# A hybrid diffusion trunk on one core: attention behind eight projection halves instead of twelve, sixteen halves in thirds between its steps, the mod group among the scan's levels

## The chip, the cores and the metric

One core of a Trainium2 chip runs the whole program. The metric is the device time of one execution in microseconds (us), the median of several runs.

## The reference, cut to what matters

Two token groups, 128 context tokens and 256 latent tokens on a 4 x 64 grid, go together (384 tokens) through two layers. A layer is a half-step SwiGLU, a token mixer and another half-step SwiGLU; each is normed before and after and modulated by shift, scale and gate from a conditioning vector. The first layer's mixer, the even mixer, is what the change touches:

```python
a_q, a_ff, a_fb, a_i, a_g, b_q, b_k, b_v = split_even(h @ w_in)      # 8 parts of 512 columns
o_a, _ = hgrn2_mixer(a_q, a_ff, a_fb, a_i, a_g, lb, gnorm, s_ctx)    # 4 heads, forward and backward gated scan
o_b = neighbourhood_attention(b_q, b_k, b_v, k_ctx, v_ctx, rpb)      # 8 heads of 64, softmax with a bias table
out = concatenate([o_a, o_b], axis=-1) @ w_out
```

For the context tokens the attention is a plain softmax over 128 keys; for the latent tokens the keys are the 256 latent ones in a window plus 128 cached ones. The new keys and values of the context tokens are outputs (cache_k_new, cache_v_new), as are the final scan states.

## The kernel before, in words

**Matmuls in three terms.** Everything is float32 with products in fp32r: each operand is split into a high part (rounded) and a low part (the rest), and a product is high x high + high x low + low x high. A weight tile is 1024 x 256; its two column halves are *halves*, numbered by tau (tile tau // 2). ScalarE makes a half's high part (L400, `split_act`), VectorE then its low part (L414, `split_dve`), and TensorE runs 24 matmuls (8 chunks x 3 terms, L445 to L447, `pe_half`). High and low parts have room for four halves, so the split of half tau + 4 waits until half tau is used. ScalarE's and VectorE's `proj(tau)` therefore each start with the split for the tile two ahead (`ahead`). For the value parts (a_i and b_v, parts 3 and 7) the tokens are the rows of the result: TensorE takes both halves of a tile at once (L1830 to L1832; it needs both low parts), and ScalarE evicts and splits the next tile's two halves only at the odd tau.

**Loads.** SyncE's DMA queue loads weight tiles of 1 MB into a ring of 6 in the order of `ring_order`; a slot's next load waits until its tile was split or, for a mod tile, used.

**Order of the even mixer's parts.** `AB_ORDER` is the order of the 16 column tiles: b_q (4 halves), b_k (4), b_v (4), then the scan's two forget parts, its query, a_i and a_g. Halves 0 to 3 run as the stage's first four, 4 to 11 by a loop, with these between them: the transposes of the cached keys (behind half 5), two pairs of slots of the mod group modC (behind 6 and 8; each 64 small matmuls, L1591), the transposes of the new context keys KP into bank 7 (behind 8), and modC's turn (behind 10). For b_q and b_k, VectorE also subtracts the high copy from the bank to get the low part (`proj_low`: BQL L1300 and L1301, KPL and BKL L1304 and L1305; semaphore proj_lo). ctx_lo (L1335) is the same for the cached keys: VectorE does it in its loop at tau 7, behind its proj(7).

**Attention steps.** The 24 units u are 8 heads x 3 query blocks. TensorE's step s runs: the scores of units s and s + 1 if s is even (L1873), the values (P x V) of step s - 3 at u % 6 of 1 or 5 (L1881, L1888), the transposes of unit s - 2 (L1918, they wait for p_ready and for the previous copy), then a part of a projection half. VectorE's step s adds the bias (L1347), takes the maximum (L1351) and scales it (L1354) for u = s, then takes the reciprocal and scales the weights of u = s - 1 (L1359, L1361), then runs its proj. ScalarE copies the transposed weights of s - 2 (L924), takes the exponent of u = s (L929), and runs its proj. Twelve halves (12 to 23) are spread over the steps, one half over two steps, 12 matmuls each, in banks 0 and 1 by turns. In step 16 ScalarE also runs four sigmoids over the forget parts (`gate_sigmoids`, L889 and L891), each side of them a table load; halves 20 and 21 run whole in steps 16 and 17, and steps 18 and 19 have none. VectorE scales the sigmoids (`gate`, L1318 and L1320) at the end of step 17 and clamps (L1324) in steps 20 and 22.

**Levels.** Behind the steps come the diagonal products and seven levels of the scan (L1931, L1964). Each level: ScalarE joins keys (L950), TensorE multiplies, VectorE updates keys, queries and totals (L1412, L1417, L1401). A projection half (24 to 31) stands behind each level. Heads, output projection and turnover follow.

Of the kernel before, what the change touches and what calls it, by code (L numbers as in the profile page):

```python
# [45 lines left out]
SIGMOIDS = (16,)  # L46
# [60 lines left out]
MOD_BANK = {6: 6, 7: 5, 8: 6, 12: 6, 16: 6, 17: 6}  # L107
# [27 lines left out]
def ring_order():  # L135
# [5 lines left out]
    for s in range(6):  # L141
# [3 lines left out]
        if kind == "even":  # L145
            order += run(f"in{s}", 2, 6) + run("modC", 0, 2) + run(f"in{s}", 6, 7) + run("modC", 2, 4)
            order += run(f"in{s}", 7, 16) + run(f"out{s}", 0, 4)
# [35 lines left out]
def trunk(nc, x_prompt, x_sample, c, state_hgrn, cache_k, cache_v, c_ctx, mod_w, mod_b, norm_pre, norm_post,  # L183
# [5 lines left out]
    with ctx:  # L189
# [20 lines left out]
        LMASK = sb("LMASK", [P, LEVELS * P], I32)[:, 0:INNER * BLK].rearrange("p (l t) -> p l t", l=INNER)  # L210
# [49 lines left out]
        KP = SUMS[:, 0:512].rearrange("p (a b) -> p a b", a=4)  # L260
# [123 lines left out]
        AB_ORDER = [10, 11, 12, 13, 14, 15, 2, 3, 4, 5, 0, 1, 6, 7, 8, 9]  # L384
# [125 lines left out]
        def ab_bank(tau):  # L510

            return bank[tau % 4 if tau < 12 else tau % 2 if tau < 24 else 4 + tau % 4]
# [15 lines left out]
        def attention_proj(step):  # L528

            part = 4 * (step % 2)  # L530
            if any(step in (at, at + 1) for at in SIGMOIDS):
                return 12 + step // 2 + step % 2, range(KD)
            if any(step in (at + 2, at + 3) for at in SIGMOIDS):
                return None
            return 12 + step // 2, range(part, part + 4)
# [61 lines left out]
        def _(pool):  # L597
# [35 lines left out]
            pool.wait_ge(kout_turned, 1)  # L633
            pool.wait_ge(mod_turned, turned_before(first_group("modC")) + 1)
# [26 lines left out]
        def _(act):  # L661
# [184 lines left out]
            def even(s):  # L846
# [47 lines left out]
                for tau in range(12):  # L894
# [7 lines left out]
                    if tau == 9:  # L902
                        act.wait_ge(kout_turned, 1)
                        act.activation(KOUT, bank[7][:], ACT.Copy).then_inc(kout_ready, 1)
                        act.wait_ge(kout_ready, 1)
                        act.dma_start(cache_k_new[0, 0].rearrange("h t d -> t h d"),
                                      KOUT.rearrange("p (h d) -> p h d", h=HEADS_B)).then_inc(k_stored, 16)
                        mod_rows_out(g0)
                mod_cols_out(g0)
                act.wait_ge(proj_out, 12)  # L910
                act.dma_start(cache_v_new[0, 0].rearrange("h t d -> t h d"),
                              BV[:, 0, :].rearrange("p (h d) -> p h d", h=HEADS_B)).then_inc(v_stored, 16)
                for step in range(24 + 3):
                    u = step - 2
                    if 0 <= u < 24:
                        n = NT if head_block(u)[1] else P
                        act.wait_ge(p_turned, u + 1)
                        if u == 0:
                            act.wait_ge(k_stored, 16)
# [17 lines left out]
                    if 2 <= step <= 24 and step % 2 == 0:  # L937
                        proj(11 + step // 2)
                    if step in SIGMOIDS:
                        gate_sigmoids(0)  # L940
                        gate_sigmoids(1)
# [12 lines left out]
                for lv in range(LEVELS):  # L954
                    join(lv)
                    if lv == 0:
                        act.wait_ge(diag_mm, 3)
                        act.activation(ATTD, level_bank(2)[:, 0:UNITS * BLK].rearrange("p (u t) -> p u t", u=UNITS),
                                       ACT.Copy).then_inc(diag_out, 1)
                    if lv == 6:  # L960
# [5 lines left out]
                    proj(24 + lv)  # L966
                act.wait_ge(lvl_mm, 3 * LEVELS)
# [22 lines left out]
                for h in range(HEADS_A):  # L990
# [6 lines left out]
                    act.wait_ge(o_mm, h + 1)  # L997
                    if h >= 2:
# [63 lines left out]
        def _(dve):  # L1062
# [223 lines left out]
            def even(s):  # L1286
# [8 lines left out]
                def proj_low(tau):  # L1295
                    part, q = divmod(AB_ORDER[tau // 2] * 2 + tau % 2, 4)
                    B = bank[tau % 4]
# [29 lines left out]
                for tau in range(12):  # L1327
# [9 lines left out]
                for step in range(24 + 1):  # L1337
# [748 lines left out]
```

## Time and profile before

| what | us |
|---|---|
| median of 3 runs | 1601.13 (1598.25 to 1602.56) |
| profiled execution, its time | 1599.43 |
| its span | 1597.4 |
| TensorE matmul busy | 1543.8 |
| VectorE busy | 1085.6 |
| ScalarE busy | 688.0 |
| even mixer: first four halves end, attention starts, levels start, levels end | 343, 385, 467, 518 |

Times in the trace count from the start of the span. In a timeline row the first number is the start, the second the length; a matmul's length is more than its distance to the next one, since they are pipelined. A bracket at the end of a row gives the idle time of the engine before it and what ended it. The clock of TensorE is the share of 2.4 GHz that was granted.

### The profile page before, as it was taken

The page shows a single profiled execution, that of the slowest core. Times are in us where ns is not written, and L with a number is a line of the kernel's source. Part 1 is how long each engine was busy: PE and PEld are TensorE (multiplying, and loading weights), DVE is VectorE, ACT ScalarE, POOL GpSimd, SP SyncE. Part 2 cuts the span into 40 slices and gives each one's busy share as a digit, 9 for nine tenths or more (in the row PEclk, how much of TensorE's full clock was granted, in tenths as well). Part 3 has the DMA queues.
Part 4 walks back from the last instruction along what each step waited for, and adds up shares of the span by engine and source line. Part 5 has one row for each costly group of instructions (what it writes and reads, how often), then busy time and mean ns, then how long its engine had stood idle before and what let it go on. Part 6 is the DMA issues. An engine that isn't in the chain of part 4 may idle for free.

```text
span 1597.4 us, 26083 instructions
## 1 busy us (share of the span) xinstructions
PE 1543.8 (97%) x10631; PEld 1508.4 (94%) x10631; DVE 1085.6 (68%) x1975; ACT 688.0 (43%) x1202; POOL 50.3 (3%) x50
## 2 busy tenths in 40 slices
PE   5999999999989899999999999999999999999999
PEld 4999999989868889999999999999999989999999
DVE  5678889774679887878946788885553885344332
ACT  4433334464556574333334533334453265333333
POOL 2000000002102000000000000000000000000000
PEclk9999999999999999999999999999999999999999
DMA  9765656567321265655645455654453354443311
GB/s 326 249 201 169 199 184 224 185 218 217 94 89 55 79 199 165 204 185 179 201 149 193 159 176 192 197 189 161 142 182 126 106 181 137 132 133 125 104 62 39
DMA packets 255654, 259.77 MB, mean 163 GB/s; under 512 B 6625, under 2 KB 253842, under 8 KB 255538
## 3 DMA queue, kind: packets, MB, share of 16 engines
q1 hardware_dynamic: 250528, 253.25, 49.1%
q10 hardware_dynamic: 4114, 2.84, 0.6%
q0 software_dynamic: 896, 2.06, 0.5%
q8 instruction: 82, 1.34, 0.4%
q14 instruction: 34, 0.28, 0.0%
HBM read 255.50 MB, written 2.62 MB: 162 GB/s over the span
## 4 chain that ended last, share of the span: by engine, by line
PE 83%; DVE 9%; ACT 3%; issue 3%; POOL 1%; ACTq 0%; DMA 0%; DVEq 0%; POOLq 0%
PE bank L445 25%; PE bank L446 24%; PE bank L447 24%; DVE PARTS L1123 1%; DVE WL L414 1%; PE bank L467 1%; PE bank L1649 1%; ACT WH L400 1%; PE bank L469 1%; PE bank L468 1%; DVE X L1189 1%; DVE HL L1152 1%; DVE SUMS L1454 1%; POOL WL L414 1%; PE bank L1830 1%
## 5 line engine op out<-in xcount | busy, mean ns | idle before, releaser
L414 DVE TENSOR_TENSOR WL<-RAW,WH 128x1024 fp32r<-128x1024 f32 (+1 forms) x335 | 398.5, 1194 | 420.4 <-ACT WH L400 419.6
L400 ACT ACTIVATE WH<-RAW 128x1024 fp32r<-128x1024 f32 (+1 forms) x344 | 357.5, 1043 | 607.0 <-PE bank L447 593.3
L445 PE MATMUL bank<-HH,WH 128*128 128x384 f32 x1664 | 564.5, 339 | 7.9 <-DVE WL L414 3.5
L447 PE MATMUL bank<-HH,WL 128*128 128x384 f32 x1664 | 561.0, 337 | 0.0
L446 PE MATMUL bank<-HL,WH 128*128 128x384 f32 x1664 | 560.9, 337 | 0.0
L445 PEld LDWEIGHTS bank<-HH,WH 128*128 128x128 f32 x1664 | 314.7, 189 | 10.0 <-issue 3.9
L446 PEld LDWEIGHTS bank<-HL,WH 128*128 128x128 f32 x1664 | 314.5, 189 | 0.0
L447 PEld LDWEIGHTS bank<-HH,WL 128*128 128x128 f32 x1664 | 314.4, 189 | 0.0
L445 PE MATMUL bank<-AH,WH 128*128 128x384 f32 x704 | 237.4, 337 | 0.0
L447 PE MATMUL bank<-AH,WL 128*128 128x384 f32 x704 | 237.0, 337 | 0.0
L446 PE MATMUL bank<-AL,WH 128*128 128x384 f32 x704 | 237.0, 337 | 0.0
L1123 DVE SCALAR_TENSOR_TENSOR SUMS<-RAW,COND,SUMS 128x256 f32<-128x256 f32 x420 | 176.2, 478 | 0.0
L445 PEld LDWEIGHTS bank<-AH,WH 128*128 128x128 f32 x704 | 132.8, 189 | 0.1
L446 PEld LDWEIGHTS bank<-AL,WH 128*128 128x128 f32 x704 | 132.8, 189 | 0.0
L447 PEld LDWEIGHTS bank<-AH,WL 128*128 128x128 f32 x704 | 132.8, 189 | 0.0
L828 ACT ACTIVATE AH<-TT 128x384 fp32r<-128x384 f32 x88 | 45.6, 519 | 108.8 <-DVE TT L1261 108.8
L467 PE MATMUL bank<-HH,WH 128*128 128x384 f32 x192 | 66.8, 348 | 4.5 <-DVE HL L1152 2.9
L469 PE MATMUL bank<-HH,WL 128*128 128x384 f32 x192 | 64.8, 337 | 0.0
L468 PE MATMUL bank<-HL,WH 128*128 128x384 f32 x192 | 64.7, 337 | 0.0
L741 ACT ACTIVATE HH<-TT,MOD,CA 128x128 fp32r<-128x128 f32 x96 | 47.3, 540 | 33.3 <-DVE TT L1138 31.8
L1123 DVE SCALAR_TENSOR_TENSOR PARTS<-RAW,COND,PARTS 128x256 f32<-128x256 f32 x140 | 56.3, 478 | 0.0
L414 POOL TENSOR_TENSOR WL<-RAW,WH 128x1024 fp32r<-128x1024 f32 x9 | 21.4, 2393 | 1085.9 <-ACT WH L400 876.6
(249 smaller groups left out, 1465.0 us busy)
## 6 DMA issues: line engine op xcount, KB each, us to landing
RAW<-in_ffn_w_in SPq DMA_DIRECT2D x88, 1024.0 KB, 5.1
RAW<-in_mod_w SPq DMA_DIRECT2D x72, 1024.0 KB, 5.0
RAW<-in_ffn_w_out SPq DMA_DIRECT2D x32, 1024.0 KB, 5.1
RAW<-in_ab_w_in SPq DMA_DIRECT2D x16, 1024.0 KB, 6.4
RAW<-in_ffn_w_out SPq DMA_DIRECT2D x16, 768.0 KB, 4.5
RAW<-in_cv_w_in SPq DMA_DIRECT2D x12, 1024.0 KB, 5.2
RAW<-in_ab_w_out SPq DMA_DIRECT2D x4, 1024.0 KB, 5.1
RAW<-in_cv_w_out SPq DMA_DIRECT2D x4, 1024.0 KB, 5.2
```

The costliest lines, as they stand in the source:

```text
L400: e.activation(WH[:, (2 * m + b) % 4, 0:nk, :], RAW[:, p, 0:nk, b * P:(b + 1) * P], ACT.Copy).then_inc(half_hi, 1)
L414: e.tensor_tensor(WL[:, k, 0:nk, :], RAW[:, p, 0:nk, b * P:(b + 1) * P], WH[:, k, 0:nk, :].bitcast(F32), ALU.subtract).then_inc(half_ready, 1)
L445: e.matmul(out, WH[:, k, kk, :], xh(kk), start=(first and kk == 0), stop=False)
L446: e.matmul(out, WH[:, k, kk, :], xl(kk), start=False, stop=False)
L447: mm = e.matmul(out, WL[:, k, kk, :], xh(kk), start=False, stop=(last and kk == nk - 1))
L467: e.matmul(outs[b], WH[:, kh[b], kk, :], HH[:, kk, :], start=False, stop=False)
L468: e.matmul(outs[b], WH[:, kh[b], kk, :], HL[:, kk, :], start=False, stop=False)
L469: e.matmul(outs[b], WL[:, kh[b], kk, :], HH[:, kk, :], start=False, stop=False)
L741: a = act.activation(HH[:, d, t0:t1], TT[:, d % 2, t0:t1], ACT.Identity, bias=MOD[:, 24 * s + d, g:g + 1], scale=CA[:, s, d, g:g + 1])
L828: act.activation(AH[:, bass.ds(i * 6 + (j + b), 1), :], TT[:, 2 + b:3 + b, :], ACT.Copy).then_inc(act_hi, 1)
L1123: x = dve.scalar_tensor_tensor(a[:, g, :], w, by, a[:, g, :], ALU.mult, ALU.add)
L1152: dve.tensor_tensor(HL[:, d, :], TT[:, 2 + d % 2, :], HH[:, d, :].bitcast(F32), ALU.subtract).then_inc(h_ready, 1)
```

## The change

The order of the tiles becomes b_q and b_k of the first four heads (halves 0 to 3), b_v (4 to 7), b_q and b_k of the other four heads (8 to 11), then as before. Attention starts behind half 7. Sixteen halves (8 to 23) run between its steps: in steps 0 to 17 two halves over three steps (18, 15 and 15 matmuls), halves 20 and 21 whole in steps 18 and 19, 22 and 23 in two parts each in steps 20 to 23. Banks 0 and 1 take turns from half 8 on, and halves 10 to 13 also wait for the low part of the half two before. The sigmoids move to step 18 (ScalarE), the gates to step 19, the clamps to 21 and 23 (VectorE). The mod group's pairs move behind levels 0 and 2, its turn behind level 4, in bank 3; the transposes of KP stand behind half 24, and KP gets a place of its own. POOL's bias loads wait for the cached keys' transposes instead of the new keys'. The ring's order follows.

```diff
-SIGMOIDS = (16,)
+SIGMOIDS = 18
-MOD_BANK = {6: 6, 7: 5, 8: 6, 12: 6, 16: 6, 17: 6}
+MOD_BANK = {6: 6, 7: 3, 8: 6, 12: 6, 16: 6, 17: 6}
-            order += run(f"in{s}", 2, 6) + run("modC", 0, 2) + run(f"in{s}", 6, 7) + run("modC", 2, 4)
-            order += run(f"in{s}", 7, 16) + run(f"out{s}", 0, 4)
+            order += run(f"in{s}", 2, 13) + run("modC", 0, 2) + run(f"in{s}", 13, 14) + run("modC", 2, 4)
+            order += run(f"in{s}", 14, 16) + run(f"out{s}", 0, 4)
-        KP = SUMS[:, 0:512].rearrange("p (a b) -> p a b", a=4)
+        KP = MASK_AREA[:, INNER * BLK:INNER * BLK + 512].bitcast(F32).rearrange("p (a b) -> p a b", a=4)
-        AB_ORDER = [10, 11, 12, 13, 14, 15, 2, 3, 4, 5, 0, 1, 6, 7, 8, 9]
+        AB_ORDER = [10, 12, 14, 15, 11, 13, 2, 3, 4, 5, 0, 1, 6, 7, 8, 9]
-            return bank[tau % 4 if tau < 12 else tau % 2 if tau < 24 else 4 + tau % 4]
+            return bank[tau % 4 if tau < 8 else tau % 2 if tau < 24 else 4 + tau % 4]
+        def fill(step):
+            if step >= SIGMOIDS + 2:
+                part = 4 * (step % 2)
+                return [(12 + step // 2, range(part, part + 4))]
+            if step >= SIGMOIDS:
+                return [(2 + step, range(KD))]
+            m, r = divmod(step, 3)
+            return [[(8 + 2 * m, range(0, 6))], [(8 + 2 * m, range(6, 8)), (9 + 2 * m, range(0, 3))],
+                    [(9 + 2 * m, range(3, 8))]][r]
+        def filled(step):
+            if step > SIGMOIDS + 2:
+                return [11 + step // 2] if step % 2 == 0 else []
+            if step > SIGMOIDS:
+                return [1 + step]
+            m, r = divmod(step - 2, 3)
+            return [8 + 2 * m + r] if step >= 2 and r < 2 else []
...
-            pool.wait_ge(kout_turned, 1)
-            pool.wait_ge(mod_turned, turned_before(first_group("modC")) + 1)
+            pool.wait_ge(ctx_turned, 1)
+            pool.wait_ge(mod_turned, turned_before(first_group("modC")))
...
-                for tau in range(12):
+                for tau in range(8):
                     proj(tau)
...
-                    if 2 <= step <= 24 and step % 2 == 0:
-                        proj(11 + step // 2)
-                    if step in SIGMOIDS:
+                    for tau in filled(step):
+                        proj(tau)
+                    if step == SIGMOIDS:
                         gate_sigmoids(0)
                         gate_sigmoids(1)
...
                     proj(24 + lv)
+                    if lv == 3:
+                        mod_rows_out(g0)
+                    if lv == 5:
+                        mod_cols_out(g0)
...
-                    if 2 <= step <= 24 and step % 2 == 0:
-                        proj(11 + step // 2)
-                    if step - 1 in SIGMOIDS:
+                    for tau in filled(step):
+                        proj(tau)
+                        if AB_ORDER[tau // 2] // 2 in (5, 6):
+                            proj_low(tau)
+                    if step == SIGMOIDS + 1:
                         for w in range(2):
                             dve.wait_ge(sig_done, 2 * w + 1)
                             gate((KFW, KBW)[w], w, k=True)
...
-                    if step in (20, 22):
-                        clamp((FF, FB)[step // 2 - 10])
-                    if step == 4:
-                        coefficients(g0)
+                    if step in (SIGMOIDS + 3, SIGMOIDS + 5):
+                        clamp((FF, FB)[(step - SIGMOIDS) // 2 - 1])
...
+                    if lv == 6:
+                        coefficients(g0)
...
                     else:
-                        pe.wait_ge(proj_out, tau - 1 if tau in range(14, 24) else tau - 3)
-                    if tau in range(4, 12):
+                        pe.wait_ge(proj_out, tau - 1 if tau in range(10, 24) else tau - 3)
+                    if tau in range(4, 8):
                         pe.wait_ge(proj_lo, tau - 3)
+                    if tau in range(10, 14):
+                        pe.wait_ge(proj_lo, tau - 5)
...
-                for tau in range(4, 12):
+                for tau in range(4, 8):
                     proj(tau)
...
-                    if tau in (6, 8):
-                        mod_pair("modC", tau - 6)
-                    if tau == 10:
-                        mod_turn(g0)
...
-                pe.wait_ge(proj_lo, 8)
+                pe.wait_ge(proj_lo, 4)
                 pe.wait_ge(ctx_lo, 1)
-                pe.wait_ge(kout_ready, 1)
...
+                        if u == 12:
                             pe.wait_ge(proj_out, 12)
-                            pe.wait_ge(mod_cols, g0 + 1)
+                            pe.wait_ge(proj_lo, 8)
...
-                    if step < 24 and attention_proj(step):
-                        proj(*attention_proj(step))
+                    for tau, steps in fill(step) if step < 24 else ():
+                        proj(tau, steps)
...
                 proj(24)
+                pe.wait_ge(ob_done, 4)
+                for ht in range(4):
+                    mm = pe.transpose(bank[7][:, ht * P:(ht + 1) * P], KP[:, ht, :], IDENT[:])
+                mm.then_inc(kout_turned, 1)
...
                     proj(25 + lv)
+                    if lv in (0, 2):
+                        mod_pair("modC", lv)
+                    if lv == 4:
+                        mod_turn(g0)
```

ScalarE's copy of the turned keys (KOUT) and its DMA to cache_k_new move from its tau 9 into level 0, and the wait for that store moves to the heads.

## Rows read from the trace of the kernel before

**Rows 1.** The page, busy time: engine, busy us, share of the span, instructions.

```profile
PE 1543.8 (97%) x10631; PEld 1508.4 (94%) x10631; DVE 1085.6 (68%) x1975; ACT 688.0 (43%) x1202; POOL 50.3 (3%) x50
```

**Rows 2.** Waits of TensorE, 343 to 518 us: us in total, times, longest.

```profile
PE bank L1918 <- DVE TT L1361: 4.8, 5, 2.0
PE bank L1931 <- ACT TT L950: 1.6, 1, 1.6
PE bank L445 <- DVE BQL L1301: 1.2, 1, 1.2
PE bank L1888 <- ACT SUMS L924: 1.1, 1, 1.1
PE bank L1918 <- ACT SUMS L924: 1.1, 1, 1.1
PE bank L1873 <- ACT MIX L859: 0.8, 1, 0.8
PE bank L1918 <- ACT SQ L924: 0.7, 1, 0.7
```

**Rows 3.** Windows: stretch, its length, busy us (instructions) per engine, clock, DMA.

```profile
445.00:450.00 5.00, 3.25 (x17) 2.04 (x19) 3.48 (x11) 3.92 (x11) 0.00 (x0) 0.72 0.00 0
...
495.00:500.00 5.00, 5.00 (x22) 5.00 (x21) 5.00 (x9) 3.33 (x5) 0.00 (x0) 0.66 0.41 135
...
550.00:555.00 5.00, 3.73 (x21) 3.20 (x20) 2.34 (x4) 3.64 (x8) 0.00 (x0) 1.00 0.00 0
```

**Rows 4.** Timeline of VectorE, 344 us: start, length, line, operands.

```profile
344.14 0.28 DVE L1300 TENSOR_TENSOR BQL<-bank,BQH 128x128 fp32r<-128x128 f32 x1
344.34 0.42 DVE L1301 TENSOR_TENSOR BQL<-bank,BQH 128x256 fp32r<-128x256 f32 x1
344.67 1.22 DVE L414 TENSOR_TENSOR WL<-RAW,WH 128x1024 fp32r<-128x1024 f32 x1
```

**Rows 5.** Timeline of TensorE and VectorE, attention's start, and the ctx_lo subtraction.

```profile
383.75 0.28 PE L1832 MATMUL bank<-WL,HH 128*128 128x256 f32 x1
...
385.91 2.36 DVE L414 TENSOR_TENSOR WL<-RAW,WH 128x1024 fp32r<-128x1024 f32 x2 [6.49 <-ACT WH L400]
...
367.10 0.68 DVE L1335 TENSOR_TENSOR BKL<-bank,BKH 128x512 fp32r<-128x512 f32 x1
```

**Rows 6.** Timeline, step 2: first scores, ScalarE's and VectorE's split.

```profile
389.65 0.45 PE L1873 MATMUL bank<-BKH,BQH 64*128 64x384 f32 x2
...
392.30 1.05 ACT L400 ACTIVATE WH<-RAW 128x1024 fp32r<-128x1024 f32 x1
...
393.38 1.23 DVE L414 TENSOR_TENSOR WL<-RAW,WH 128x1024 fp32r<-128x1024 f32 x1 [1.27 <-ACT WH L400]
```

**Rows 7.** Timeline around the sigmoids: a half's first and last matmul, ScalarE, VectorE.

```profile
438.26 0.42 PE L445 MATMUL bank<-HH,WH 128*128 128x384 f32 x1
...
442.33 0.34 PE L447 MATMUL bank<-HH,WL 128*128 128x384 f32 x1
...
436.48 1.28 ACT L889 ACT_TABLE_LOAD   x1
...
442.20 1.48 ACT L891 ACTIVATE MIX<-MIX 128x1536 f32<-128x1536 f32 x1
...
444.08 1.28 ACT L929 ACT_TABLE_LOAD   x1
...
439.30 1.41 DVE L1318 TENSOR_SCALAR MIX<-MIX,LBT 128x384 f32<-128x384 f32 x4 [0.31 <-ACT MIX L889]
...
443.72 1.65 DVE L1320 TENSOR_SCALAR MIX<-MIX,LBT 128x384 f32<-128x384 f32 x4
```

**Rows 8.** Timeline of TensorE, one pair of mod slots.

```profile
357.97 1.96 PE L1591 MATMUL bank<-RAW,COND 128*32 128x128 f32 x64
```

**Rows 9.** Windows, the levels, columns as in rows 3.

```profile
476.00:518.00 42.00, 39.55 (x821) 37.35 (x820) 40.14 (x69) 26.43 (x43) 8.17 (x4) 0.96 0.16 53
```

More of the change, by code:

```diff
@@ L209, in trunk @@
         ONES = sb("ONES", [P, P])
-        LMASK = sb("LMASK", [P, LEVELS * P], I32)[:, 0:INNER * BLK].rearrange("p (l t) -> p l t", l=INNER)
+        MASK_AREA = sb("LMASK", [P, LEVELS * P], I32)
+        LMASK = MASK_AREA[:, 0:INNER * BLK].rearrange("p (l t) -> p l t", l=INNER)
         WINDOW = sb("WINDOW", [P, GRID_W])
@@ L526, in weights_of @@
             return (SQ, SQ_ODD)[h % 2][:, (i + 1) % 2, :]
[L528 to L535, printed above, removed]
+        def fill(step):
[14 more added lines that the diff above has]
+            return [8 + 2 * m + r] if step >= 2 and r < 2 else []
         def two_halves(t, other, at, blocks, b, left=0, right=None):
@@ L901, in even @@
                                        ACT.Copy).then_inc(ctx_ready, 1)
[L902 to L910, printed above, removed]
+                act.wait_ge(proj_out, 8)
                 act.dma_start(cache_v_new[0, 0].rearrange("h t d -> t h d"),
@@ L917, in even @@
                         act.wait_ge(p_turned, u + 1)
-                        if u == 0:
-                            act.wait_ge(k_stored, 16)
                         if u % 6 >= 4:
@@ L959, in even @@
                                        ACT.Copy).then_inc(diag_out, 1)
+                        act.wait_ge(kout_turned, 1)
+                        act.activation(KOUT, bank[7][:], ACT.Copy).then_inc(kout_ready, 1)
+                        act.wait_ge(kout_ready, 1)
+                        act.dma_start(cache_k_new[0, 0].rearrange("h t d -> t h d"),
+                                      KOUT.rearrange("p (h d) -> p h d", h=HEADS_B)).then_inc(k_stored, 16)
                     if lv == 6:
@@ L997, in even @@
                     act.wait_ge(o_mm, h + 1)
+                    if h == 0:
+                        act.wait_ge(k_stored, 16)
                     if h >= 2:
@@ L1296, in proj_low @@
                     part, q = divmod(AB_ORDER[tau // 2] * 2 + tau % 2, 4)
-                    B = bank[tau % 4]
+                    B = ab_bank(tau)
                     dve.wait_ge(proj_out, tau + 1)
@@ L1326, in even @@
                 g0 = first_group("modC")
-                for tau in range(12):
+                for tau in range(8):
                     proj(tau)
@@ L1811, in proj @@
                     elif tau == 27:
-                        pe.wait_ge(ob_done, 4)
+                        pe.wait_ge(kout_ready, 1)
                     else:
-                        pe.wait_ge(proj_out, tau - 1 if tau in range(14, 24) else tau - 3)
-                    if tau in range(4, 12):
+                        pe.wait_ge(proj_out, tau - 1 if tau in range(10, 24) else tau - 3)
+                    if tau in range(4, 8):
                         pe.wait_ge(proj_lo, tau - 3)
+                    if tau in range(10, 14):
+                        pe.wait_ge(proj_lo, tau - 5)
                     part = AB_ORDER[tau // 2] // 2
@@ L1847, in even @@
                         mm.then_inc(ctx_turned, 1)
-                    if tau in (6, 8):
-                        mod_pair("modC", tau - 6)
-                    if tau == 10:
-                        mod_turn(g0)
-                    if tau == 8:
-                        pe.wait_ge(proj_out, 8)
-                        for ht in range(4):
-                            mm = pe.transpose(bank[7][:, ht * P:(ht + 1) * P], KP[:, ht, :], IDENT[:])
-                        mm.then_inc(kout_turned, 1)
-                pe.wait_ge(proj_lo, 8)
+                pe.wait_ge(proj_lo, 4)
                 pe.wait_ge(ctx_lo, 1)
-                pe.wait_ge(kout_ready, 1)
                 def scores(u):
@@ L1896, in even @@
                         if u == 0:
-                            pe.wait_ge(proj_out, 11)
+                            pe.wait_ge(proj_out, 7)
                         if u == 2:
+                            pe.wait_ge(proj_out, 8)
+                        if u == 12:
                             pe.wait_ge(proj_out, 12)
-                            pe.wait_ge(mod_cols, g0 + 1)
+                            pe.wait_ge(proj_lo, 8)
                         if u >= 4:
@@ L1907, in even @@
                         if u == 1:
-                            pe.wait_ge(proj_out, 12)
+                            pe.wait_ge(proj_out, 8)
                         if u % 6 == 1 and u > 1:
```

## The prediction, made before the changed kernel ran

> **What bounds the kernel now.** I read the page first, then who waited for whom on TensorE around the even mixer, then the timeline there, all engines side by side. TensorE is busy 97% of the span [rows 1], so a change of order can only change TensorE's idle time and its clock. In 343 to 518 us, from the mixer's fifth half to the end of its levels, that is little: the waits of [rows 2] sum to 11.3 us. Four (4.8 + 1.1 + 1.1 + 0.7 = 7.7 us) lie between attention steps, 0.7 of it in the early steps, 3.1 behind the sigmoids (1.1 and 2.0), 4.0 in the last steps. The other three: 1.2 before the fifth half, 0.8 before the first scores, 1.6 before level 3.
>
> The second loss is the clock. Behind the idle time of 443 to 447 us the granted clock is 0.72 for 5 us, behind the 1.6 us before level 3 it is 0.66 [rows 3]: a mix of the levels 2.4 and 1.2 GHz. Prices: 0.28 x 5 = 1.4 us, with the end of the drop 1.5, and 0.34 x 5 = 1.7 us. Yet in 550 to 555 us TensorE idles 1.3 us and the clock stays at 1.00 [rows 3], so a drop is likely and not sure.
>
> **The change, step by step.** TensorE's work stays the same: halves, scores, values, transposes and the mod group only change places. So I sum idle and slow time after minus before, over the same stretch. A half is 24 matmuls, 438.26 to the last start 442.33, that is 4.24 us with its switch; 12 more matmuls cost 2.1 us [rows 7].
>
> *A, the fifth half.* It becomes a V half, which needs both low parts of tile 2 instead of one. Before, TensorE left at the end of the first low-part subtraction, 344.76; the second split runs from 344.67 for 1.22 us [rows 4], so it leaves at 345.9. Price **+1.1**.
>
> *B, ctx_lo.* TensorE waits for ctx_lo before the first scores. VectorE issues it behind its proj(7). That tile is now V: its two low splits wait for ScalarE's two high splits, which wait for TensorE's half 7. Nothing is left in front of TensorE then. The same chain stands in the trace behind half 11: TensorE's last matmul 383.75 + 0.28 = 384.03, VectorE's pair of low splits ends at 385.91 + 2.36 = 388.27, 4.2 us later; the ctx_lo subtraction adds 0.68, less 0.1 of overlap [rows 5]. So 4.8 us of idle, where 0.8 stood [rows 2]. Price **+4.0**: four halves covered it before, nothing does now. From above 4.8, with no bound near 0, since every link of the chain is in the rows.
>
> *C, two banks.* Halves 8 to 11 used four banks and now use two, and two halves on wait for the low part (proj_lo) too. 16 matmuls a step are 2.8 us instead of 2.1. For half 10, due in step 3: from the scores of step 2 (389.65 before) ScalarE's split starts at 392.30 and VectorE's ends at 393.38 + 1.23 = 394.61 [rows 6]; the two BQL subtractions of half 8 add 0.6 [rows 4], so it is free 5.5 us after those scores start. TensorE is there after 0.7 + 0.1 + 2.6 + 0.1 = 3.5: idle 2.0. The same for half 12 (three evictions, then KPL and BKL) gives 0.7; halves 14 and 18, behind steps with the two output copies, about 0.6 and 0.5. Sum 3.8, before 0.7: **+3.1**. From below: halves 14 to 21 alternate in two banks before, without a wait before a half there in [rows 2], which gives -0.7; from above, twelve halves that wait 0.6 each give +6.5. I take the chain, since it follows the order of the queues. Perfetto Trace Analysis of the Trainium skill (Optimizing Tensor Performance, Matmuls) wants independent matmul groups to rotate through different PSUM banks so that evacuation overlaps: by it C is a loss, while by the quiet alternation of before the sum would be 3.8 us less.
>
> *D, the sigmoids.* They move from step 16 to 18, and halves 20 and 21 run whole beside them as before; the two empty steps behind are now filled with half 22. But VectorE's gates come behind its proj(20), the low split of tile 12's first half, and ScalarE makes the high split only in its step 19, behind all sigmoids. Before, the gates ran under the sigmoids: the first at 439.30, the last at 443.72 [rows 7]. Counted from the first table load S (436.48): sigmoids end at +7.2 (442.20 + 1.48), copy and second table load +8.9 (444.08 + 1.28) [rows 7], exponent of u=19 +9.4, high split +10.4, low split +11.6, the four groups of gates (1.41 + 1.65 twice, less overlaps, 5.9) +17.5, bias, maximum and scaling +18.9. Only then can TensorE transpose u=19 in step 21. In front of it TensorE has: half 21 to +6.1, scores to +6.9, values from +7.6 (when the copy is done and the second load starts) to +9.0, the first part of half 22 from +10.8 (half 20's eviction) to +12.9. Idle 0.7 + 1.8 + 6.0 = 8.5. The last steps keep their kind of wait; VectorE is as late as before and the clamps stand a step later: 4.1 for 4.0. So 12.6 idle after, against 7.0 idle and 1.5 of slow clock before: **+4.1**. Its own slow clock comes while ScalarE and VectorE set the pace and I let it vanish there. Bounds +1 (half 22 slow, so idle shrinks, and the tail closes) and +7 (clock not hidden). The page ScalarE: Activation LUTs of the Trainium skill (What ACT_TABLE_LOAD costs) adds a drain of 1.38 us to each switch. The rows disagree: from the load's end, 437.76, four sigmoids of 1.48 fill the time to 443.68. By the page D would be 2.8 us more.
>
> *E, clock.* The 4.8 us idle of B should bring the low clock to the first step, which TensorE bounds; price as in [rows 3], 1.5 to 1.7: **+1.6**, bounds 0 and +5 (a second drop behind the 2 us of C).
>
> *F, the levels.* The mod group's 128 small matmuls (1.96 us a pair, 1.9 start to start [rows 8]), its turn and the turn of KP move here: 4.5 us of TensorE work. VectorE is the other engine of the levels: 476 to 518 us has it busy 40.1 of 42 us, TensorE 39.6 [rows 9]. The second pair stands just before level 3 and covers its 1.6 us wait; with it the slow 1.7 goes: -3.3, less 0.2 for a thin VectorE lead: **-3.1**. Bounds -3.3 and 0: if VectorE stays later than TensorE, the new work is just added. ScalarE's copy of KOUT and the DMA issue behind it stand in front of join 1, which waits for level 0 anyway: 0.
>
> *Covered, so 0.* POOL starts its bias loads at ctx_turned, near 355, over 10 us before the second pair of scores. On SP the six weight tiles move two places forward, and modC's slots fall free at level 0, 10 us before tile 15 is split; if they were late, ScalarE's split in level 3 would wait. Mod coefficients are only needed by the turnover. k_stored is waited for some 40 us after its DMA.
>
> **Sum.** 1.1 + 4.0 + 3.1 + 4.1 + 1.6 - 3.1 = **+10.8**. The profiled execution took 1599.43 us (span 1597.4), so 1610.2. It stands 1.7 us under the median 1601.13, to which I carry the same difference: **1611.9**.
>
> **Rivals.**
> *R1, faster: the denser steps hide all.* With 16 matmuls a step no chain is late from step 3 to step 26: C -0.7, D -8.5, F -3.1, A and B +5.1, no E: -7.2, 1593.9. It decides at the transposes of u=19: they would have to be ready before the first part of half 22 ends, so the gates would have to run under the sigmoids. For it: one idle time of [rows 2] lies just there. Against: the order in VectorE's queue. Perfetto Trace Analysis of the Trainium skill (Optimization Strategy) says that interleaving regimes with different busiest engines may improve performance; that is this case. Chance 0.06.
> *R2, no change: B and A as said, the rest quiet.* C 0, D 0, E 0, F -3.1: +2.0, so 1603.1. For it: other halves alternate quietly in two banks. Chance 0.14.
> *R3, slower by more.* F gives nothing, since VectorE is full in the levels, and the low clock lasts (E +4): 10.8 + 3.1 + 2.4 = +16.3, 1617.4. For it: 40.1 of 42 us. Against: VectorE waits for level 0's matmuls even now. Chance 0.2.
> *The forecast:* chance 0.6.
>
> A measurement of this kernel tells about 0.3% from no change, 4.8 us. Low end: A and B +5.1, C 0, D +1, E 0, F -3.1 gives +3.0, 1604.1, which takes in all but R1 and a part of R2; so 1604. High end: R3 and a little, 1619. Faster 0.06, within 0.14, slower 0.8.
>
> **What would show it.** Idle before the first scores near 4.8 us, put down to VectorE's ctx_lo subtraction; a wait for BQL before half 10 of 1.5 to 2.5 us; gates that start over 10 us after the first sigmoid, and one wait of 5 to 6 us before a transpose after them; clock under 0.9 in the first 5 us of attention; no wait before level 3. If gates run beside sigmoids, D is wrong; if the attention start has no long wait, B is wrong and the sum falls to R2 or R1; if the levels take over 44 us from level 0, F is wrong.

## The result, and the profile after

The changed kernel takes 1613.57 us (median of 4 runs, 1609.78 to 1615.44), the kernel before in the same comparison 1600.48 (4 runs). The ratio is 1.0081, 95% interval [1.0067, 1.0096]: 0.8% slower, some 13 us. The forecast was 1611.9, range 1604 to 1619. The profiled execution took 1609.78 us, span 1607.8, against 1599.43 and 1597.4 before: +10.4. It is the shortest of the four, so the mechanism is read from it and the size from the medians.

The page's busy time of TensorE answers to [rows 1]: the same work and the same count, 0.9 us longer busy, 10.4 us longer span.

```profile
PE 1544.7 (96%) x10631; PEld 1509.7 (94%) x10631; DVE 1086.8 (68%) x1975; ACT 687.6 (43%) x1202; POOL 50.5 (3%) x50
```

Waits of TensorE, 343 to 530 us, the same stretch of work as [rows 2] (the levels now end at 529.1 instead of 517.3 us):

```profile
PE bank L1927 <- DVE TT L1374: 7.1, 3, 5.8
PE bank L1880 <- DVE BKL L1348: 4.9, 1, 4.9
PE bank L1847 <- DVE WL L415: 2.4, 1, 2.4
PE bank L446 <- issue: 2.2, 2, 1.8
PE bank L1895 <- ACT SUMS L926: 1.3, 2, 0.9
PE bank L446 <- ACT MIX L895: 1.3, 1, 1.3
PE bank L1848 <- issue: 1.2, 1, 1.2
PE bank L1993 <- ACT MIX L881: 0.6, 1, 0.6
PE bank L1940 <- issue: 0.5, 1, 0.5
```

In the order of time: 2.4 before the fifth half, 4.9 before the first scores, 1.8 before half 10, then 5.8 before the transposes of u=19 (L1927). Without L1993, whose 0.6 us the kernel before has too, they sum to 20.9 us where [rows 2] has 11.3. The rows whose releaser is "issue" waited for nothing that the profile names. Those of L446 are the halves 10 and 12 (1.8 and 0.4); to those of L1848 and L1940, in the levels, nothing of before answers. The 1.6 us before level 3 are gone.

Windows, columns as in [rows 3]; the last row is the levels, as [rows 9]:

```profile
365.00:370.00 5.00, 1.39 (x8) 1.30 (x9) 3.40 (x6) 2.75 (x3) 0.00 (x0) 0.59 0.36 87
370.00:375.00 5.00, 5.00 (x23) 5.00 (x22) 0.81 (x5) 0.84 (x4) 0.00 (x0) 0.73 0.52 178
380.00:385.00 5.00, 3.18 (x13) 2.91 (x13) 3.30 (x8) 2.67 (x8) 0.00 (x0) 0.79 0.00 0
385.00:390.00 5.00, 5.00 (x30) 4.33 (x30) 3.51 (x9) 1.55 (x6) 0.98 (x2) 0.87 0.49 150
460.00:465.00 5.00, 2.52 (x9) 2.52 (x10) 3.16 (x9) 2.61 (x7) 0.00 (x0) 0.64 0.00 0
465.00:470.00 5.00, 5.00 (x26) 3.94 (x26) 4.42 (x12) 1.63 (x6) 0.00 (x0) 0.67 0.62 206
...
487.80:529.80 42.00, 39.73 (x849) 37.87 (x848) 39.09 (x70) 25.56 (x44) 8.17 (x4) 1.00 0.58 183
```

The granted clock is low in three places, each behind one of the long waits (4.9, 1.8 and 5.8 us). In the levels it is now 1.00, but the loads move 183 GB/s there, against 53 in [rows 9].

The timeline, one link per line, all engines. The attention's start, as [rows 5]:

```profile
363.39 0.28 PE L1849 MATMUL bank<-WL,HH 128*128 128x256 f32 x1
...
364.46 1.06 ACT L401 ACTIVATE WH<-RAW 128x1024 fp32r<-128x1024 f32 x1
...
365.55 2.36 DVE L415 TENSOR_TENSOR WL<-RAW,WH 128x1024 fp32r<-128x1024 f32 x2 [6.47 <-ACT WH L401]
...
367.83 0.68 DVE L1348 TENSOR_TENSOR BKL<-bank,BKH 128x512 fp32r<-128x512 f32 x1
...
368.62 0.47 PE L1880 MATMUL bank<-KPH,BQH 64*128 64x128 f32 x2 [4.95 <-DVE BKL L1348]
...
379.49 1.05 ACT L401 ACTIVATE WH<-RAW 128x1024 fp32r<-128x1024 f32 x1
...
380.57 1.23 DVE L415 TENSOR_TENSOR WL<-RAW,WH 128x1024 fp32r<-128x1024 f32 x1 [1.29 <-ACT WH L401]
...
381.92 0.41 DVE L1314 TENSOR_TENSOR BQL<-bank,BQH 128x256 fp32r<-128x256 f32 x1
...
382.43 0.42 PE L446 MATMUL bank<-HH,WH 128*128 128x384 f32 x1 [1.82 <-issue]
...
444.91 1.49 ACT L901 ACTIVATE MIX<-MIX 128x1536 f32<-128x1536 f32 x1
...
453.93 1.23 DVE L415 TENSOR_TENSOR WL<-RAW,WH 128x1024 fp32r<-128x1024 f32 x1 [8.68 <-ACT WH L401]
...
455.07 1.40 DVE L1331 TENSOR_SCALAR MIX<-MIX,LBT 128x384 f32<-128x384 f32 x4
...
459.27 1.64 DVE L1333 TENSOR_SCALAR MIX<-MIX,LBT 128x384 f32<-128x384 f32 x4
...
462.48 0.47 PE L1927 MATMUL bank<-IDENT,TT 128*128 128x128 f32 x1 [5.79 <-DVE TT L1374]
```

Three readings. ctx_lo (L1348), ready since half 6, runs behind two low splits that wait for ScalarE. Half 10 (382.43) has no named releaser, but VectorE's BQL subtraction, which frees its bank, ends 0.1 us before it, and that stands behind a split nobody waited for yet. The gates start 10.2 us after the first sigmoid (444.91), 1.1 us behind the start of a low split that VectorE had waited 8.68 us for.

### The profile page after: what moved, and what is told of

Read it like the earlier page. It is cut to its first block, busy times and chain, and to the rows that moved or that the text cites. A ratio compares the mean times of both kernels' runs of the same rounds, so it can differ in the third digit from the quotient of the medians.

```text
span 1607.8 us, 26082 instructions
## 1 busy us (share of the span) xinstructions
PE 1544.7 (96%) x10631; PEld 1509.7 (94%) x10631; DVE 1086.8 (68%) x1975; ACT 687.6 (43%) x1202; POOL 50.5 (3%) x50
## 3 DMA queue, kind: packets, MB, share of 16 engines
q8 instruction: 82, 1.34, 0.4%
## 4 chain that ended last, share of the span: by engine, by line
PE 85%; DVE 9%; ACT 3%; issue 2%; POOL 1%; DMA 0%; ACTq 0%; DVEq 0%; POOLq 0%
PE bank L446 25%; PE bank L447 24%; PE bank L448 24%; DVE WL L415 1%; DVE PARTS L1136 1%; PE bank L468 1%; PE bank L1664 1%; PE bank L470 1%; PE bank L469 1%; ACT WH L401 1%; DVE X L1202 1%; PE bank L1847 1%; PE bank L1848 1%; PE bank L1849 1%; DVE HL L1165 1%
## 5 line engine op out<-in xcount | busy, mean ns | idle before, releaser
L446 PE MATMUL bank<-HH,WH 128*128 128x384 f32 x1664 | 565.1, 340 | 10.3 <-DVE WL L415 3.5
L446 PEld LDWEIGHTS bank<-HH,WH 128*128 128x128 f32 x1664 | 314.7, 189 | 13.2 <-issue 6.6
L446 PE MATMUL bank<-AH,WH 128*128 128x384 f32 x704 | 237.0, 337 | 0.0
L446 PEld LDWEIGHTS bank<-AH,WH 128*128 128x128 f32 x704 | 132.3, 188 | 0.1
```

Of the source, the lines that this page charges most:

```text
L446: e.matmul(out, WH[:, k, kk, :], xh(kk), start=(first and kk == 0), stop=False)
```

## The experiments

The first three change nothing in the changed kernel but the order inside an engine's queue (in the third, of two engines); each run is compared with the kernel before on the same chip.

**ctx_lo first.** In VectorE's loop over the first eight halves:

```diff
                 for tau in range(8):
+                    if tau == 7:
+                        dve.wait_ge(ctx_ready, 1)
+                        dve.tensor_tensor(BKL[:, :, DEC_SEQ:NT], ..., ALU.subtract).then_inc(ctx_lo, 1)
                     proj(tau)
                     if AB_ORDER[tau // 2] // 2 in (5, 6):
                         proj_low(tau)
-                    if tau == 7:
...
```

> The changed kernel with one order undone: VectorE subtracts ctx_lo ahead of its proj(7), so TensorE no longer waits for the low splits behind half 7. Theory (terms B and E): the wait before the first scores falls from 4.9 us to under 1, the clock in the first 10 us of attention stays at 1.00 instead of 0.59 and 0.73, and the time falls by 5 to 7 us against the changed kernel, to about 1607. Rival 1 (the low parts of half 8 or 9 would be late anyway): the wait moves to the first halves, the time falls by under 2 us. Rival 2 (the clock drop has nothing to do with this idle time): the wait goes, the clock still falls, and the time falls by 4 us alone.

1606.32 us, ratio 1.0038 [1.0025, 1.005]: 6.9 us less than the changed kernel by the ratios (1.0081 against 1.0038), by the later measurement of that kernel (1.0076, below) 6.1. The wait before the first scores is 0.78 us, ScalarE's copy of CV, as before the change; the clock is 1.00 from 365 to 390 us. Half 10 still waits 1.8 us, yet no drop follows it (the changed kernel measured again, below, has none there either, so that is not this edit's doing):

```profile
365.00:370.00 5.00, 4.28 (x28) 4.24 (x29) 3.07 (x6) 4.42 (x7) 0.00 (x0) 1.00 0.44 90
...
380.00:385.00 5.00, 5.00 (x35) 4.33 (x34) 4.41 (x12) 1.99 (x6) 2.03 (x4) 1.00 0.41 116
```

So this one wait costs 4.1 us of idle time and, priced in the changed kernel's profile, about 2 of slow clock behind it.

**Gates first.** In VectorE's step SIGMOIDS+1 the gates stand ahead of `for tau in filled(step)`:

```diff
+                    if step == SIGMOIDS + 1:
+                        for w in range(2):
+                            ...
                     for tau in filled(step):
                         proj(tau)
...
-                    if step == SIGMOIDS + 1:
```

> The changed kernel with VectorE's gates ahead of its proj(20) in step 19, so that they run under the sigmoids. Theory (term D): the gates start within 0.5 us of the first sigmoid's end, the wait of 5.8 us before the transpose of u=19 falls to under 1.5, and the time falls by 5 to 8 us (idle and the low clock behind it), to about 1607. Rival (ScalarE's four sigmoids and two table loads are the pace, wherever the gates stand): the wait before that transpose stays over 4 us and the time falls by under 2 us.

1606.46 us, ratio 1.0041 [1.0029, 1.0053]: 5.6 us less by the later measurement. VectorE's timeline:

```profile
447.89 1.41 DVE L1331 TENSOR_SCALAR MIX<-MIX,LBT 128x384 f32<-128x384 f32 x4 [1.17 <-ACT MIX L901]
...
452.31 1.65 DVE L1333 TENSOR_SCALAR MIX<-MIX,LBT 128x384 f32<-128x384 f32 x4
...
455.40 1.22 DVE L415 TENSOR_TENSOR WL<-RAW,WH 128x1024 fp32r<-128x1024 f32 x1 [1.44 <-ACT WH L401]
```

The gates run under the sigmoids, the wait of 5.8 us is gone, and the clock stays at 1.00 from 455 to 480. Waits of 1.1 and 1.4 us come up behind it, so the gain is less than 5.8 plus the 2.5 of slow clock.

**Evict first.** For halves 8 to 11 ScalarE evicts ahead of its high split, and VectorE subtracts ahead of its low split (the same exchange in both queues):

```diff
                     for tau in filled(step):
-                        proj(tau)
                         if AB_ORDER[tau // 2] // 2 in (5, 6):
                             proj_low(tau)
+                        proj(tau)
```

> The changed kernel with, for halves 8 to 11, ScalarE's evictions ahead of its next split and VectorE's low parts ahead of its next split. Theory (term C): the waits before half 10 (1.8 us) and half 12 (0.4 us) go, with the low clock behind the first (0.79 at 380 to 385 us); the time falls by 2 to 4 us. Rival (half 10 waits for its own weights, not for its bank): the wait stays, the time stays within 1 us or rises, as the split comes later.

1609.95 us, ratio 1.0067 [1.0054, 1.008], 1.4 to 2.2 us less than the changed kernel; the intervals overlap, so the trace decides. Half 10's wait fell from 1.82 to 0.16 us and half 12's 0.4 is gone. The clock of 380 to 390 is 1.00, but it is so in the second profile of the changed kernel too, with the wait in place, so only the waits are credited to the edit:

```profile
379.67 0.29 DVE L1318 TENSOR_TENSOR BQL<-bank,BQH 128x128 fp32r<-128x128 f32 x1 [0.79 <-ACT BQH L889]
...
380.39 0.42 PE L446 MATMUL bank<-HH,WH 128*128 128x384 f32 x1 [0.16 <-issue]
```

**The mod group alone**, in the kernel before: its pairs behind levels 0 and 2, its turn at level 4, its tiles loaded seven weight tiles later; twelve halves, sigmoids and banks stay.

```diff
-            order += run(f"in{s}", 2, 6) + run("modC", 0, 2) + run(f"in{s}", 6, 7) + run("modC", 2, 4)
+            order += run(f"in{s}", 2, 13) + run("modC", 0, 2) + run(f"in{s}", 13, 14) + run("modC", 2, 4)
...
                     proj(25 + lv)
+                    if lv in (0, 2):
+                        mod_pair("modC", lv)
+                    if lv == 4:
+                        mod_turn(g0)
```

> The kernel before with one part of the change alone: the mod group's pairs behind levels 0 and 2, its turn behind level 4, and the ring's order to match; the attention and its halves stay as before. Theory (term F): the wait of 1.6 us before level 3 and the low clock behind it go, the time falls by 2 to 3.5 us against the kernel before, to about 1597.5. Rival (VectorE is full in the levels, TensorE's new work is just added there and its old place gives nothing back beyond that): no change within 1 us.

1597.51 us, ratio 0.9988 [0.9979, 0.9996]. The wait before level 3 and its slow clock are gone, 3.3 us, and two pauses are new (1.2 and 0.6 us), as in the changed kernel:

```profile
485.96 0.38 PE L1833 MATMUL bank<-WH,HL 128*128 128x256 f32 x1 [1.15 <-issue]
...
503.00 0.64 PE L1928 MATMUL bank<-MIX,TT 128*32 128x32 f32 x49 [0.60 <-issue]
```

**All three moves together**, in the changed kernel.

> The changed kernel with the three reorderings together: ctx_lo ahead of proj(7), gates ahead of proj(20), evictions and low parts ahead of the splits for halves 8 to 11. Theory: the three are in different stretches and add: -6.3, -6.1 and -2.7 from the changed kernel's 1612.6, so about 1597.5, within 0.3% of the kernel before and like it with the mod group's move alone. Rival (they share the same slack): under two thirds of the sum, above 1602.

1597.93 us, ratio 0.9989 [0.998, 0.9997]. The three add up, and the result equals the mod group alone. TensorE's waits up to the end of the levels sum to 11.6 us in both profiles: between the attention's steps 6.2 instead of 7.8, but 2.4 instead of 1.2 before the fifth half, which no move touches, and 2.2 instead of 1.8 of pauses. So the early attention's loss sat in those three places of the queues, but for 1.2 us before the fifth half; the 1.6 us that the denser steps bring pay for that, and nothing measurable is left over.

**The pauses.** First theory: weight loads that now run in a burst of 4 MB through the levels. One run spreads them over the levels (SP waits for lvl_mm ahead of five of them, in the version with the mod group alone), one does the same in the version with all three moves, and one puts a burst into the kernel before, by holding the first tile of ab_w_out until two levels are done (4 MB then run from 484 to 497 us).

```diff
                 wait_ring(place[st, n])
+                if (st, n) in HOLD:
+                    sp.wait_ge(lvl_mm, HOLD[st, n])
                 load(st, n, *src_of(st, n))
```

> The kernel before with the mod group in the levels, and SyncE's loads of the output tiles and of the next stage's first two tiles held back to one per level, where they ran as bursts of 3 and 4 MB at over 340 GB/s. Theory (TensorE's pauses of 1.2 and 0.6 us inside a half and inside level 5's matmuls, which wait for nothing that the profile shows, come from its instructions arriving late behind such a burst): both pauses go, -1 to -2 us from 1597.5. Rival (they come from the many small matmuls of the mod pairs themselves, a matter of count): the pauses stay, no change within 1 us.

> The kernel before with nothing moved, only the four loads of the output tiles held until level 1's matmuls are done, so that they run as one burst of 4 MB in the levels. Theory (late instructions): a pause of TensorE of 0.5 to 1.3 us that waits for nothing shown appears in the levels behind the burst, where the kernel before has none. Rival (count of small matmuls): no such pause. The time may rise by 0 to 1.5 us in either case, so the waits of the trace decide.

> The changed kernel with the three reorderings and the loads held apart. Theory: 1 to 2 us under the three reorderings alone, about 1596, so 0.2 to 0.3% under the kernel before. Rival: as the three alone.

Loads apart: 1598.93, 0.9991 [0.9983, 1.0]; three pauses, 2.1 us, in other places. Burst in the kernel before: 1601.14, 1.0001 [0.999, 1.0012]; one pause of 0.26 us. All three moves, loads apart: 1598.36, 0.9996 [0.9987, 1.0005]; 2.0 us. Spreading was a miss: the pauses were to go, and stayed. The burst alone does little, one pause shorter than the 0.5 to 1.3 us expected. But the three pauses had moved with the loads:

```profile
488.00 0.38 PE L1836 MATMUL bank<-WH,HL 128*128 128x256 f32 x1 [0.83 <-issue]
...
493.77 0.70 PE L1931 MATMUL bank<-MIX,TT 128*32 128x32 f32 x57 [0.52 <-issue]
...
500.07 0.66 PE L1931 MATMUL bank<-MIX,TT 128*32 128x32 f32 x51 [0.72 <-issue]
```

Between them TensorE issues 126 matmuls and as many weight loads, to within one; between the two pauses of the changed kernel it is 378, three times 126. Counted from the start of the program, all 26 such pauses in the levels, over the profiles of all 13 kernel runs other than the kernel before, stand at the 3480th, 3607th, 3733rd or 3860th matmul, to within two, whatever the kernel computes there. That is a block of instructions. The page's queues (queue, kind: packets, MB, share) have one for them, and 0.1 us windows of the DMA view give each packet's start; here 498.50 to 498.60 us of the changed kernel, weight loads on q1 beside it:

```profile
q8 instruction: 82, 1.34, 0.4%
...
q1 hardware_dynamic: 31, 0.03, 100.6%
q8 instruction: 1, 0.02, 67.9%
```

82 packets of 1.34 MB are 16 KB each, and 1.34 MB over TensorE's 2 x 10631 instructions is 63 bytes for one: I take the queue to be TensorE's. Counting every 126 matmuls from a pause gives the other blocks (in the kernel before, the same counts from the program's start):

| kernel | TensorE enters the block before | packet starts | next block's first matmul | pause |
|---|---|---|---|---|
| changed | 495.13 | 498.5 | 501.17 | 1.18 |
| changed | 511.75 | 515.6 | 518.21 | 0.51 |
| mod group alone | 479.95 | 483.3 | 485.96 | 1.15 |
| loads apart | 488.01 | 491.2 | 493.77 | 0.52 |
| burst, kernel before | 489.37 | 493.2 | 495.93 | 0.26 |
| all three moves | 498.56 | 503.4 | 505.92 | 1.43 |
| changed | 501.17 | 502.9 | 506.24 | none |
| changed | 518.21 | 522.1 | 525.67 | none |
| before | 487.60 | 488.9 | 493.65 | none |
| before | 493.65 | 494.3 | 500.90 | none |
| all three moves, loads held (last run) | 498.49 | 499.3 | 504.24 | none |

Where there is a pause, the first matmul comes 2.5 to 2.7 us behind its packet's start, so a block is in time if it lasts longer than the third column less the second, plus 2.6. With no load under way (the rows of before) the packet starts 1.3 and 0.7 us after TensorE enters the block before; ahead of every pause, with loads under way, 3.2 to 4.8 us. The first row: 3.4 + 2.6 = 6.0 us for a block whose matmuls take 6.04 - 1.18 = 4.9. The two rows without a pause in the changed kernel ran beside loads too: one packet started after 1.7 us (1.7 + 2.6 is under the block's 5.1), the other after 3.9 (6.5, under 7.5). A block of a half's matmuls lasts 126 / 24 x 4.2 = 22 us, far more than the longest delay seen, 4.8 + 2.7 = 7.5 us. The last run tests it, in the version with all three moves:

```diff
                 wait_ring(place[st, n])
+                if (st, n) == ("out1", 2):
+                    sp.wait_ge(lvl_mm, 3 * LEVELS)
                 load(st, n, *src_of(st, n))
```

> All three moves, and SP holds the third tile of ab_w_out, and so every load behind it, until the last level's matmuls are done: of the loads in the levels the last tile of ab_w_in and two of ab_w_out are left. What was read from the traces before this run: TensorE's own instruction blocks come by the DMA queue named 'instruction', one 16 KB packet per 126 matmuls and their 126 weight loads. Every pause without a releaser stands at such a block's first instruction, 2.3 to 2.7 us behind the start of its packet; with no load under way the packet starts 0.6 to 1.3 us behind TensorE's step into the block before, with loads under way 3.1 to 4.8 us. Theory 'late instruction block': in the version with all three moves the pause of 0.8 us stays, since its packet starts in the loads that are left, the pause of 1.4 us (packet at 503.4, in the second burst) goes: 1.4 us less than that version (1597.9), so about 1596.5, ratio 0.998. Rival 'the added small matmuls pause by themselves': about 2.2 us of pauses stay, same time as that version. Rival 'loads held are loads late': both pauses change as said, but a wait for a weight split appears behind the levels and the time stays or grows.

1597.18 us, ratio 0.9984 [0.9975, 0.9993], the lowest of all. Of the pauses above 0.2 us one is left, the one that was to stay, and behind the levels no new wait came up:

```profile
487.90 0.39 PE L1855 MATMUL bank<-WH,HL 128*128 128x256 f32 x1 [0.88 <-issue]
```

The pause of 1.4 us went as said, and the table's last row has the reason: no load runs from 491 to 510 us, and that block's packet starts 0.8 us after TensorE enters the block before, where it took 4.8. A pause's length is not the same in every version, though: at this place it is 0.8 and 0.4 us in the two variants of the three moves that follow. The time, 0.7 us lower in the median where 1.4 was expected, agrees in direction, but the intervals overlap: the pause is shown, its microsecond in the total is not.

**Half 20 and the filled halves; the changed kernel again.** In the version with all three moves, ScalarE evicts half 20 as well ahead of its split, or every filled half.

```diff
-                    if tau not in range(8, 12):
+                    if tau not in (*range(8, 12), 20):
                         halves_ahead[tau % 2]()
```

> All three moves, and ScalarE evicts half 20 ahead of its high split too, for the wait of 1.3 us before half 22. Theory 'VectorE sets the pace from the gates to u=23': the wait before half 22 shrinks by the split's 1.05 us to about 0.3, the waits of the transposes behind it grow by the same, the time stays at 1597.9 (0.9989). Rival 'each wait is worth its own length': the others stay, 1596.9 (0.998).

> All three moves, and ScalarE evicts every filled half ahead of its high split. Theory: between the steps no half but 10, 12 and 20 waited for its bank, so this frees nothing more; the weight splits come 0.5 us later and have several us of lead: the same time as the version with half 20 alone, within 0.5 us. Rival: late splits become waits for the low part (VectorE's WL) before halves, +1 us or more.

> The changed kernel once more, beside the runs of this batch, so that the gains of the three moves are read against it and not across batches. All theories agree: ratio 1.008 to the kernel before, with the waits of 4.9 us before the first scores, 1.8 us before half 10 and 5.8 us before the transposes of u=19 where they were.

Half 20: 1598.41, 0.9996 [0.9987, 1.0005]. The wait before half 22 shrinks, the transposes take it over (before the edit 1.3 and 3.3):

```profile
PE bank L1934 <- DVE TT L1381: 4.7, 4, 1.4
...
PE bank L446 <- ACT MIX L900: 0.4, 1, 0.4
```

So VectorE sets the pace there, as expected. All filled halves: 1598.86, 0.9994 [0.9985, 1.0003], nothing more, as expected. The changed kernel again: 1612.14, ratio 1.0076 [1.0062, 1.0089], the waits of 4.9, 1.8 and 5.8 us where they were. Two things differ between these two profiles of one kernel: the pauses are 0.9 and 1.0 us instead of 1.2 and 0.5, and the clock behind the same waits is another, 0.83 and 0.50 instead of 0.59 and 0.73 in the first step, and 1.00 instead of 0.79 behind the 1.8 us before half 10:

```profile
365.00:370.00 5.00, 1.53 (x8) 1.44 (x9) 3.55 (x6) 2.71 (x4) 0.00 (x0) 0.83 0.38 94
370.00:375.00 5.00, 5.00 (x17) 5.00 (x17) 0.66 (x4) 0.74 (x4) 0.00 (x0) 0.50 0.49 172
...
380.00:385.00 5.00, 3.18 (x19) 2.91 (x19) 3.58 (x9) 2.67 (x8) 0.00 (x0) 1.00 0.00 0
```

## Why the prediction was right

The time, the side and the largest terms were right. Three terms were off by 1.5 to 2 us, one over and two under, so that part of the closeness is their cancelling. Idle plus slow time, after minus before, in the profiled executions:

| term | predicted | measured | from |
|---|---|---|---|
| A, fifth half | +1.1 | +1.2 | wait 2.4 for 1.2 |
| B, ctx_lo | +4.0 | +4.1 | 4.95 for 0.8 |
| C, two banks | +3.1 | +1.5 | half 10 1.8, half 12 0.4, for 0.7 |
| D, sigmoids | +4.1 | +3.8 | idle 9.8, slow 2.5, for 8.5 |
| E, clock | +1.6 | +3.5 | 1.9 in the first step, 1.6 behind half 10 |
| F, levels | -3.1 | -1.6 | wait 1.6 and slow 1.7 gone, pauses 1.7 new |
| sum | +10.8 | +12.5 | span +10.4, medians +13.1 |

*A and B* hold link by link; the ctx_lo chain of [rows 5] repeats to 0.1 us, and the first experiment shows that the order in VectorE's queue is the whole of it.

*C is over-sized.* The step that failed is "halves 14 and 18, behind steps with the two output copies, about 0.6 and 0.5": no half from 13 to 21 waited for its bank (half 22's wait is part of D), and half 12 waited 0.4 instead of 0.7. The estimate for half 10, 2.0 us, measured 1.8. I had carried the same chain on to halves 14 and 18, although the kernel before showed halves 14 to 21 quiet in two banks, which was the lower bound. The rule on rotating banks (Perfetto Trace Analysis of the Trainium skill, Optimizing Tensor Performance) called C a loss, and the trace agrees in sign: two waits, 1.8 and 0.4 us. An exchange in the queues removed them with the two banks kept.

*D is right in size, in part by luck.* Gates 10.2 us after the first sigmoid and one wait of 5.8 before u=19 are as predicted. But "I let it vanish there" was wrong for the slow clock: behind the 5.8 us half 22's last 12 matmuls took 4.2 us for 2.3, 2.5 us in all with the scores. The tail's waits were smaller than the 4.1 taken over from before (0.5, 0.8, 0.9), and that paid for it. The table load shows no drain: in the changed kernel too it takes 1.28 us (443.61 to 444.89) and the sigmoid starts at 444.91. The 1.38 us of the Trainium skill (ScalarE: Activation LUTs, What ACT_TABLE_LOAD costs) are not in this trace either.

*E is under-sized.* It had one drop; in this profile there were two. "A second drop behind the 2 us of C" stood as a bound only. Whether it comes differs from execution to execution: in the second profile of the same kernel the 1.8 us before half 10 were followed by a clock of 1.00, and the first step's drop cost 2.8 us (0.17 x 1.5 + 0.50 x 5.0), so E is 3.5 in one profile and 2.8 in the other.

*F is over-sized.* "The second pair stands just before level 3 and covers its 1.6 us wait; with it the slow 1.7 goes: -3.3" held to the letter, and no wait for VectorE took its place. What failed is the step under *Covered, so 0*: the weight tiles that move "two places forward" (tiles 6 and 13 do; the six between them move four, past both pairs of modC) were costed by when their slots fall free, and not by what their traffic does beside 128 more small matmuls. It makes two instruction blocks late, 1.2 + 0.5 us. The mod group alone measures the whole term: 0.9988 x 1600.5 is 1.9 us less.

*The sum of the rows is 2.1 us over the profiled difference.* Some 1.4 of it is a slow clock behind the attention's end in the profile of before, which I had not read and which the profile after does not have; priced by TensorE's busy time there, 0.24 x 3.8 + 0.10 x 5.0:

```profile
465.00:470.00 5.00, 3.76 (x111) 2.48 (x111) 4.02 (x6) 2.87 (x6) 0.91 (x1) 0.76 0.29 97
470.00:475.00 5.00, 5.00 (x54) 4.94 (x46) 5.00 (x8) 2.04 (x4) 0.01 (x1) 0.90 0.68 223
```

It belongs to no part of the change: with ctx_lo first such a drop appeared (0.93, 0.50 and 0.89 from 465 to 480 us), with gates first and with evict first it did not. The other 0.7 us is not assigned. Drops that come in one execution and not in another also bear on the medians: the three executions of the changed kernel that were not profiled have a mean granted clock of 0.989 to 0.990 and take 1612.6 to 1615.4 us, the profiled one 0.993 and 1609.8. So that the forecast, worked out from one profile, lies within 2 us of the median is in part luck.

*The rivals.* R1 decided at gates under the sigmoids; they ran behind. With all three moves it does come true in that point, and gives 1598, not 1594, since from the sigmoids on six waits of 0.5 to 1.4 us stay, 6.0 us in all, where R1 had none. R2 wanted C, D and E quiet: D and E were not. R3 wanted VectorE to hold the levels back; no wait for VectorE stands there. Its other half, the longer low clock, did come in part (3.5 and 2.8 in the two profiles, for its 4).

## What to carry to other kernels

When a piece of work is moved, look on each in-order queue for what stands behind the instruction that will now wait: the three losses here were short, long-ready operations (a subtraction of 0.7 us, four gates, an eviction) queued behind a weight split that waited for another engine, and putting them ahead of it gave back all of the 0.8%. In these traces a wait of 5 to 6 us on TensorE cost about half as much again in slow clock behind it (1.9 and 2.8 us behind the 4.95, 2.5 behind the 5.8). And where matmuls are small, count instructions: a stretch that uses up a block of them in 5 us should not have weight loads under way when the next block is fetched.

## What the runs showed of the hardware that was not expected

- As far as these traces show it, TensorE's instructions arrive by DMA in 16 KB blocks (here 126 matmuls with their weight loads) on a queue of its own. Beside weight loads (270 to 360 GB/s on average from entry to packet, 308 or more ahead of every pause) the packet starts 1.7 to 4.8 us after TensorE has entered the block before, without loads 0.7 to 1.3 us, and pauses of 0.3 to 1.4 us without a releaser are its trace. That the request waits behind queued load packets fits this, but only the start of the packet is seen.
- The same idle time is not always followed by a low clock, not even in the same kernel: 1.8 us before half 10 by 0.79 in one profile of the changed kernel and by 1.00 in the other. The 2.4 us before the fifth half stand in ten profiles; in five of them the clock of 345 to 350 us is 0.66 to 0.73, in the other five 1.00. What decides it stays open; a drop's coming or going in a single profile is no effect of an edit.
